# Other slots for the side steps of a two-layer mixer kernel on one core

## The reference, cut to what matters

```python
u = _rmsnorm(h, norm_w)
proj = jnp.matmul(u, w_in.astype(jnp.float32))
...
h_a = _mlstm_chunkwise(_heads(ml_q, ML_HEADS), _heads(ml_k, ML_HEADS),
                       _heads(ml_v, ML_HEADS), i_pre, logf)
...
qkv = _causal_conv_silu(dn_qkv, dn_conv_w)
dq = _l2norm(_heads(dq, DN_HEADS))
dk_ = _l2norm(_heads(dk_, DN_HEADS))
h_b = _gated_delta_chunkwise(dq, dk_, dv_, beta, g)      # solves (I + A) X = ...
h_b = _merge_heads(_rmsnorm(h_b, dn_norm_w)) * jax.nn.silu(dn_z)
...
return jax.nn.sigmoid(gate_a) * y_a + jax.nn.sigmoid(gate_b) * y_b
```

## Time and profile before

| | us |
|---|---|
| times | 2036.54, 2039.27, 2039.55 |
| median | 2039.27 |
| the profiled execution | 2042.45 |
| its span in the trace | 2040.6 |
| TensorE busy | 1953.3 (96%) |
| VectorE busy | 1389.8 (68%) |
| ScalarE busy | 952.0 (47%) |
| GpSimd busy | 248.0 (12%) |
| TensorE's granted clock, mean | 0.987 |

### The profile page before, as it was taken

One profiled execution on the slowest core, in us unless ns is written; L12 is line 12 of the kernel. 1 busy time (PEld: TensorE's weight loads), 2 busy tenths in 40 slices (PEclk: granted clock), 3 DMA queues, 4 the chain that ended last, 5 costly groups with the idle time before them and its releaser, 6 DMA issues.

```text
span 2040.6 us, 29310 instructions
## 1 busy us (share of the span) xinstructions
PE 1953.3 (96%) x11910; PEld 1719.4 (84%) x11910; DVE 1389.8 (68%) x1943; ACT 952.0 (47%) x1352; POOL 248.0 (12%) x425
## 2 busy tenths in 40 slices
PE   5999999999999999999999999999999999999997
PEld 5988888877888898987888788989898998988885
DVE  4676667675788888888777648674455567656574
ACT  5555555553533333434444446563333355545443
POOL 1006061614011101011111000000000000011000
PEclk9999999999999999999999999999999999999999
DMA  6445353544688888685877876666656533544553
GB/s 210 133 147 163 107 156 109 150 128 148 209 279 269 271 263 259 198 269 171 309 260 269 267 237 199 207 193 204 189 173 191 156 128 124 170 145 129 187 184 124
DMA packets 184663, 392.22 MB, mean 192 GB/s; under 512 B 12568, under 2 KB 12848, under 8 KB 183376
## 3 DMA queue, kind: packets, MB, share of 16 engines
q1 hardware_dynamic: 166240, 321.95, 49.4%
q0 software_dynamic: 17424, 66.72, 10.8%
q10 hardware_dynamic: 864, 1.67, 0.2%
HBM read 386.08 MB, written 4.22 MB: 191 GB/s over the span
## 4 chain that ended last, share of the span: by engine, by line
PE 77%; DVE 11%; ACT 5%; issue 4%; POOL 1%; DMA 1%; SPq 0%; ACTq 0%; DVEq 0%; POOLq 0%
PE GB L1954 44%; PE GB L1958 24%; DVE WL L1902 3%; ACT WH L1898 2%; DVE yth L680 2%; DVE macc L1278 1%; PE SB L352 1%; PE SB L1584 1%; PE SB L1296 1%; POOL TB L980 1%; PE SB L1576 1%; POOL XB L983 1%; DMA wm<-in_w_mod 1%; PE SB L742 1%; DMA xin<-in_x 1%
## 5 line engine op out<-in xcount | busy, mean ns | idle before, releaser
L1902 DVE TENSOR_TENSOR WL<-raw,WH 128x1024 fp32r<-128x1024 f32 x608 | 738.5, 1234 | 286.3 <-ACT WH L1898 283.6
L1898 ACT ACTIVATE WH<-raw 128x1024 fp32r<-128x1024 f32 x608 | 627.8, 1057 | 423.9 <-PE GB L1954 284.6
L1954 PE MATMUL GB<-WH,uH 128*128 128x512 f32 x896 | 284.1, 398 | 1.7 <-DVE WL L1902 1.7
L1954 PE MATMUL GB<-WH,uL 128*128 128x512 f32 x896 | 278.5, 392 | 0.0
L1954 PE MATMUL GB<-WL,uH 128*128 128x512 f32 x896 | 277.8, 391 | 0.0
L1958 PE MATMUL GB<-uH,WH 128*128 128x256 f32 x1280 | 217.6, 293 | 3.8 <-DVE WL L1902 3.8
L1278 DVE SCALAR_TENSOR_TENSOR macc<-wm,csil,macc 128x512 f32<-128x512 f32 x300 | 209.5, 749 | 5.2 <-DMA wm<-in_w_mod 4.1
L1958 PE MATMUL GB<-uL,WH 128*128 128x256 f32 x1280 | 209.1, 287 | 0.0
L1958 PE MATMUL GB<-uH,WL 128*128 128x256 f32 x1280 | 207.9, 285 | 0.0
L1954 PEld LDWEIGHTS GB<-WH,uL 128*128 128x128 f32 x896 | 169.5, 189 | 36.3
L1954 PEld LDWEIGHTS GB<-WL,uH 128*128 128x128 f32 x896 | 169.4, 189 | 36.2
(11 more groups left out here) (397 smaller groups left out, 2214.1 us busy)
## 6 DMA issues: line engine op xcount, KB each, us to landing
raw<-in_w_in SPq DMA_DIRECT2D x512, 512.0 KB, 4.3
wm<-in_w_mod POOLq DMA_DIRECT2D x96, 512.0 KB, 5.8
raw<-in_w_out SPq DMA_DIRECT2D x96, 512.0 KB, 5.1
xin<-in_x SPq DMA_DIRECT2D x4, 512.0 KB, 6.6
E<-decay_rows POOLq DMA_DIRECT2D x4, 512.0 KB, 5.5
hres<-in_x POOLq DMA_DIRECT2D x1, 2048.0 KB, 11.4
cin<-in_ctx POOLq DMA_DIRECT2D x1, 2048.0 KB, 8.4
h_spill<-hres POOLq DMA_DIRECT2D x2, 1024.0 KB, 5.6
```

Source lines behind the costliest of these rows:

```text
L1898: e.activation(WH[s % NH][:, :, :], raw[s % NR][:, :, :], ACT.Copy).then_inc(*wh.inc("WH", s))
L1902: e.tensor_tensor(WL[s % NH][:, :, :], raw[s % NR][:, :, :], f32(WH[s % NH][:, :, :]), sub).then_inc(*wl.inc("WL", s))
L1954: m = e.matmul(banks[j][:, :], x[:, c, 128 * j:128 * j + 128], w[:, k, :], start=first, stop=last, skip_group_check=True)
```

## The change

The table of slots:

```diff
-    steps("gates", 5, 13, 1.0)
+    steps("gates", 8, 13, 1.0)
...
+    for n in range(4):
+        steps(("quad", n), end("qkv", 3 * n + 2) + 7, 4)
+        steps(("quad", n), end("qkv", 3 * n + 2) + (21 if n < 3 else 22), 10)
     for k in range(12):
-        steps(("cv", k), end("qkv", k), 9 if k % 3 < 2 else 6)
-    for n in range(4):
-        steps(("quad", n), end("qkv", 3 * n + 2) + 6, 4)
-        steps(("quad", n), end("qkv", 3 * n + 2) + 20, 9)
+        steps(("cv", k), end("qkv", k), 10 if k % 3 < 2 else 6)
...
+    steps("mlrow", end("mlk", 0), 1)
     for half in range(2):
-        steps(("ml", half), end("mlv", 2 * half + 1) + 1, 7)
+        steps(("ml", half), end("mlv", 2 * half + 1) + 1, 7, 0.5)
...
-    steps("lam", end("mlz", 3) + 10, 3)
+    steps("lam", end("mlz", 3) + 10, 4)
```

The loads of the maxima for the mLSTM:

```diff
+        def maxima_pool(e, h):
+            e.dma_start(Em[:, h % 2, 0:256], rowMd[h:h + 1, :].partition_broadcast(128)).then_inc(rowM_in[h % 2], 16)
+
+        def first_maxima_pool(e):
+            e.wait_ge(*yb_dve.at("y1", 3))
+            for h in range(2):
+                maxima_pool(e, h)
+            yield
+
         def mlstm_pool(e, hf):
-            for k in range(4):
-                h = 4 * hf + k
-                if h >= 2:
-                    e.wait_ge(*mq_dve.at("p", h - 2))
-                else:
-                    e.wait_ge(*yb_dve.at("y1", 3))
-                e.dma_start(Em[:, h % 2, 0:256], rowMd[h:h + 1, :].partition_broadcast(128)).then_inc(rowM_in[h % 2], 16)
+            for k in range(5):
+                h = 4 * hf + k - 1
+                if k and h + 2 < 8:
+                    e.wait_ge(*mq_dve.at("p", h))
+                    maxima_pool(e, h + 2)
                 yield
```

More of the change, by code:

```diff
@@ L696, in conv_pe @@
                 m = 2 * n + kind
-                for _ in range(7):
+                for _ in range(8):
                     yield
@@ L710, in conv_pool @@
                 m = 2 * n + kind
-                for _ in range(8):
+                for _ in range(9):
                     yield
@@ L1077, in ml_pe @@
                 yield
-        def mlstm_pool(e, hf):
-            for k in range(4):
-                h = 4 * hf + k
-                if h >= 2:
-                    e.wait_ge(*mq_dve.at("p", h - 2))
-                else:
-                    e.wait_ge(*yb_dve.at("y1", 3))
-                e.dma_start(Em[:, h % 2, 0:256], rowMd[h:h + 1, :].partition_broadcast(128)).then_inc(rowM_in[h % 2], 16)
+        def maxima_pool(e, h):
[4 more added lines that the diff above has]
+                maxima_pool(e, h)
+            yield
+        def mlstm_pool(e, hf):
+            for k in range(5):
[3 more added lines that the diff above has]
+                    maxima_pool(e, h + 2)
                 yield
@@ L2109, in _ @@
             stages = {"mod": modulate_pool(e), "ctx": context_pool(e), "h1": h1_spill_pool(e), "attb": attend_b_pool(e),
-                      "ob": gated_b_pool(e)}
+                      "ob": gated_b_pool(e), "mlrow": first_maxima_pool(e)}
             stages["gates"] = gates_pool(e)
```

## The result

| | before | changed |
|---|---|---|
| median, us | 2039.26 | 2049.01 |
| lowest and highest | 2036.54, 2039.55 | 2047.67, 2052.91 |
| profiled execution | 2042.45 | 2049.93 |
| its span | 2040.6 | 2048.1 |

A forecast was written before the change was run, and what follows sets the result against it. It took TensorE's idle waits and time at its lower clock as the bound. Quads +16.5, rest of slots 0 to 131 +0.8, heads -6.9, lambda -5.4 gave +5.0: 2047.5 us profiled, 2044.3 median, range 2032 to 2053.

The forecast's parts named there:

- y5, quads 0 to 2: Step y5 of a quad's solve: wait 1.8 us instead of 1.51, +0.3 a quad, ends 0 and +1.4.
- z5: Step z5 of a quad's solve: longer queue behind X, wait 5.2 us where 2.9 was, +2.4 a quad.
- The sums behind z5: Sums L702, moved behind z5, wait for two PSUM banks its copies must have left: +0.9 us a quad.
- Transposes: Transposes of values (L733) wait for bank 0 behind the earlier quad's normalisation: 3.8 us instead of 3.2, +0.6 a quad.
- The clock: TensorE's lower clock after a z5 wait of 5 us instead of 3: +0.5 us a quad.
- Quad 3: Last quad: y5's wait goes (-7); z gate +3.8, clock +2, next matrix's transposes +2.3; together +1.1 us.
- First transposes and gates: Quad 0's first transposes gain one slot in part, -1.5 us; gates from slot 8 instead of 5, 0 (2.5 either way).
- Heads: mLSTM heads get two slots each: waits of 5.2 and 1.7 us at products behind late splits go, -6.9.
- Lambda: L1227 one product back: its wait falls to 0.4 us and the half-rate product behind it goes, -5.4.
- The first rival: l2 step doesn't delay scaling L645: a quad costs 2.5 us, total -4.0, 2035; chance 0.22.
- The rival that quads cost less: No GpSimd collision, no z6 effect, banks free for the sums: a quad costs 3.5 us, 2038; chance 0.18.
- The third: Rival: late weights replace lambda's wait and half the heads' gain is lost, +8.9 on the sum, 2053; chance 0.1.

The follow-up runs named there:

- e3_l2: The changed kernel with the l2 norm's sums, Ln, Exp and multiply back in their old slots: 2036.10 us, 0.9981 of before.
- e2_xt: The changed kernel with XT directly behind X again and VectorE's copy of y5 one split earlier: 2041.83 us, 1.0005 of before.
- e6_order: e1_rest with the quad's step taken ahead of the convolution's in the slot behind y5, no slot changed: 2016.26 us, 0.9892 of before.
- e4_banks: The changed kernel with the transposes of the values written to small banks 1 and 2 instead of 0 and 1: 2052.20 us, 1.0061 of before.
- e1_rest: The changed kernel with quads, l2 norm and gates back in their old slots; heads, maxima and lambda stay changed: 2024.71 us, 0.9927 of before.
- e5_masks: e1_rest with value transposes in banks 1 and 2, normalised output a step later, next quad's masks and Exp a slot earlier: 2025.91 us, 0.9937 of before.
- e9_vv: e1_rest with value transposes in banks 1 and 2, normalised output later, masks directly behind it, values taken with the last taps: 2015.43 us, 0.9883 of before.

## Why the prediction was right, and by how much it was short

It forecast slower by 5.0 us in the sum of the profiled execution; the trace has 7.5.

- **y5, quads 0 to 2:** waits of 1.9, 1.6 and 1.4 us against 1.8. X was to start 8.9 to 10.0 us after slot 44; it started at 9.75. The scaling ended 6.3 us after slot 40 rather than 5.7 (before it was 3.8, not 3.6). The ends of this term are misworked: waits of 1.2 and 2.3 us against 1.51 are -0.3 and +0.8, not 0 and +1.4. The split beside GpSimd's multiply took 0.58 us more than usual: it stood still for the last 0.7 us of the multiply and then took its 1.09, as in the earlier trace rows. It is the rule of the Trainium skill's "SBUF — State Buffer", section "Who interferes with whom" (a port pair held as an exclusive lock for the whole instruction), and this trace agrees with it. I had it collide by half without a reason; that this came out is luck, since the split happened to begin late in the multiply (in e3_l2 it began earlier and took 2.14 us). e3_l2 shows the cause of the late scaling.
- **z5:** forecast 5.2 us, measured 5.32. e2_xt took one split away from the chain and got 1.2 us of wait for it; e6_order took out the taken k and its square, and got nearly all.
- **The sums behind z5:** 0.96 us against 0.9. **z6:** 0.7 to 1.1 against 0.8. **Transposes:** 3.94, 3.94 and 4.08 against 3.8, and by e4_banks for the reason given, bank 0; of the 2.8 us more that a drain would have cost there is nothing.
- **The clock was the term that was mis-sized.** For a longer wait at z5 it was +0.5 us a quad. The waits themselves came out: the forecast adds 5.0 us of them to a quad (0.3 + 2.4 + 0.9 + 0.8 + 0.6), and TensorE is idle for 5.1, 5.1 and 4.9 us more in quads 0, 1 and 2. But with the same matmuls it is also busy for 2.4, 2.0 and 2.4 us longer, where +0.5 stood. The rows that carry it are the sums (3.75 us against 1.88) and the product behind them. I had priced the clock by the length of z5's wait alone; but the sums and their wait follow it directly, so that nearly everything from 198 to 210 stood still or ran at the lower rate, and the longer wait at the transposes had its own share. Three quads are 21.8 us where 17.7 were forecast, with the 1.2 us for quad 2's masks behind the z gate; these did not come (no wait at the key products between slots 92 and 116), or the miss would be larger.
- **Quad 3:** +2.0 against +1.1, with the waits as named: y5 none, z5 3.7, the transposes of the next matrix 2.1. A wait of 1.4 us at the first product with that matrix (575.35 us) was not in the forecast. **First transposes and gates:** -1.5 as forecast (-2.04 less 0.5 at the start), but by luck: the wait at the first transposes fell from 2.9 to 1.8 us and 0.5 came at the key products, so that the slot gave some 0.5; the rest is the clock between slots 24 and 44, which e1_rest had too with the old slots. The gates' zone is even, as forecast. What the later gates saved at the sums came back as waits of products for late splits (7.6 us in six, L1972, where 3.8 in two were).
- **Heads:** -9.1 against -6.9. Their waits went as forecast, 5.2 us, and of those at products behind late splits 0.5 are left. That is the 6.9 us of idle time; the other 2.2 are busy time of TensorE, at full clock in both. A part is that each wait cost 0.2 us more than its idle time: a slot with a head's step took 5.5 us without a wait and 7.05 with one of 1.30. The rest is not traced.
- **Lambda:** -5.3 against -5.4.
- **Median:** the profiled execution of before lay 3.2 us above its median, and I carried that over; the changed kernel's lies 0.9 above. That is 2.3 of the 4.7 us between 2044.3 and 2049.0. The rest is the 7.5 us of the traces against 5.0. This sum agreed better than its parts, which is luck: the quads took 5.0 us more than forecast (4.1 in quads 0 to 2, 0.9 in quad 3), and the heads gave 2.2 us more.

The first rival (the l2 step doesn't delay the scaling) is refuted by the two lines of ScalarE above. The rival that quads cost less fell on the other side. The third (the gains don't come) is refuted by e1_rest.

## What to carry to other kernels

Count a step's lateness in queue entries, not in slots: a step that is given two slots more and put behind two more entries of the same queue has gained nothing, and one that changes places with its neighbour within a slot can gain it all (e6_order, 8.5 us). A wait can have more than one root; before removing the one that the trace names, follow what stands behind it in the same queue, because it can be late next (e4_banks and e5_masks gained nothing, e9_vv 9.3 us). And split a bundle of edits: this one held 15 us of gain under 24 us of loss.

## What was not expected of the hardware

The same idle time was followed by a lower clock in one kernel and not in another. In the kernel before, y5 waits 1.51 us and the product behind it starts at full rate (0.74 us for four matmuls; 0.64 later). In e6_order y5 waits 1.51 us too, and four matmuls behind it take 1.13 and 1.05 us, for some 3 us. What the engine had done in the two products before was alike in both. And in quads 1 and 2 of e6_order itself y5 waits 1.53 us and the clock stays full. The same shows between slots 24 and 44, where kernels with the same queues and the same wait of 2.9 us took 68.5 or 70.1 us. So what the clock takes away for one wait can't be read from another of the same length here; why, these runs leave open. And the lower clock reaches past the wait to whatever side work stands next: the sums L704 took twice their time there.
